# Second block, first pair of down projections: the three product terms outside the contraction tiles

## The reference, cut to what matters

```python
def swiglu(x, w_gate, w_up, w_down):
    return (jax.nn.silu(x @ w_gate) * (x @ w_up)) @ w_down
...
    for l in range(DEPTH_2):
        h = h + 0.5 * swiglu(rmsnorm(h, ffn1_norm[l]), ffn1_w_gate[l], ffn1_w_up[l], ffn1_w_down[l])
        ...
        h = h + 0.5 * swiglu(rmsnorm(h, ffn2_norm[l]), ffn2_w_gate[l], ffn2_w_up[l], ffn2_w_down[l])
```

## Time and profile before

| | |
|---|---|
| median of 3 runs | 3017.49 us (3017.19 to 3018.07) |
| the profiled execution | 3017.36 us |
| its span | 3015.6 us |
| TensorE busy | 2999.4 us |
| VectorE busy | 2122.8 us |
| ScalarE busy | 1449.4 us |
| granted TensorE clock, mean | 0.999 |

### The profile page before, as it was taken

One profiled execution on the slowest core, in us unless ns is written; L12 is line 12 of the kernel. 1 busy time (PEld: TensorE's weight loads), 2 busy tenths in 40 slices (PEclk: granted clock), 3 DMA queues, 4 the chain that ended last, 5 costly groups with the idle time before them and its releaser, 6 DMA issues.

```text
span 3015.6 us, 55700 instructions
## 1 busy us (share of the span) xinstructions
PE 2999.4 (99%) x20562; PEld 2751.3 (91%) x20562; DVE 2122.8 (70%) x3141; ACT 1449.4 (48%) x2555; POOL 190.1 (6%) x237
## 2 busy tenths in 40 slices
PE   9999999999999999999999999999999999999998
PEld 7878887888888899999999999999999999989998
DVE  5545646773576598877667788868887766788876
ACT  4454424442343365634652555536554475356642
POOL 1000000000000011100000011001110000001100
PEclk9999999999999999999999999999999999999999
DMA  4111322222222267533111477336753321257734
GB/s 163 62 64 63 105 98 99 98 97 92 97 97 97 77 181 180 149 109 106 64 64 64 140 178 184 102 112 171 187 147 112 105 71 65 70 148 188 176 105 126
DMA packets 131033, 347.94 MB, mean 115 GB/s; under 512 B 14798, under 2 KB 16334, under 8 KB 130752
## 3 DMA queue, kind: packets, MB, share of 16 engines
q1 hardware_dynamic: 103536, 292.34, 28.8%
q0 software_dynamic: 27056, 53.16, 10.4%
q10 hardware_dynamic: 288, 0.31, 0.0%
HBM read 343.58 MB, written 2.17 MB: 115 GB/s over the span
## 4 chain that ended last, share of the span: by engine, by line
PE 79%; issue 16%; DVE 3%; ACT 1%; POOL 1%; DVEq 1%; DMA 0%; POOLq 0%; SPq 0%; ACTq 0%
PE ps L3129 25%; PE ps L2704 22%; PE ps L2852 9%; PE ps L3194 6%; PE ps L2717 3%; PE ps L3483 3%; PE ps L3176 3%; PE ps L2869 1%; PE ps L2937 1%; PE ps L3261 1%; DVE w_lo L1591 0%; PE ps L2925 0%; PE ps L2906 0%; PE ps L2758 0%; PE ps L2778 0%
## 5 line engine op out<-in xcount | busy, mean ns | idle before, releaser
L865 ACT ACTIVATE w_hi<-w_raw 128x1024 fp32r<-128x1024 f32 (+1 forms) x325 | 340.6, 1048 | 567.7 <-PE ps L2704 255.1
L1591 DVE TENSOR_TENSOR w_lo<-w_raw,w_hi 128x1024 fp32r<-128x1024 f32 (+1 forms) x333 | 403.0, 1210 | 200.0 <-ACT w_hi L865 193.8
L2704 PE MATMUL ps<-h_hi,w_lo 128*128 128x512 f32 (+1 forms) x584 | 215.0, 379 | 0.0
L2704 PE MATMUL ps<-h_hi,w_hi 128*128 128x512 f32 (+1 forms) x584 | 213.8, 377 | 1.1 <-DVE w_lo L1591 0.8
L2704 PE MATMUL ps<-h_lo,w_hi 128*128 128x512 f32 (+1 forms) x584 | 213.9, 377 | 0.0
L1232 ACT ACTIVATE h_spare<-ps 128x264 f32<-128x264 f32 (+1 forms) x304 | 118.2, 389 | 130.0 <-PE ps L3129 129.8
L2852 PE MATMUL ps<-h_hi,w_hi 128*128 128x512 f32 x416 | 168.3, 405 | 0.0
L2852 PE MATMUL ps<-h_hi,w_lo 128*128 128x512 f32 x416 | 163.2, 392 | 0.0
L2852 PE MATMUL ps<-h_lo,w_hi 128*128 128x512 f32 x416 | 163.1, 392 | 0.0
L2704 PE MATMUL ps<-f_hi,w_lo 128*128 128x512 f32 (+1 forms) x520 | 154.4, 338 | 0.0
L2704 PE MATMUL ps<-f_lo,w_hi 128*128 128x512 f32 (+1 forms) x520 | 153.8, 337 | 0.0
(11 more groups left out here) (542 smaller groups left out, 7785.6 us busy)
## 6 DMA issues: line engine op xcount, KB each, us to landing
w_raw<-in_stream SPq DMA_DIRECT2D x384, 512.0 KB, 3.3
s_raw<-in_stream SPq DMA_DIRECT2D x152, 256.0 KB, 4.4
s_raw<-in_stream POOLq DMA_DIRECT2D x152, 256.0 KB, 4.1
tmp<-in_stream SPq DMA_DIRECT2D x76, 256.0 KB, 5.1
w_raw<-in_stream SPq DMA_DIRECT2D x32, 256.0 KB, 2.7
w_mix<-in_stream SPq DMA_DIRECT2D x24, 256.0 KB, 3.4
w_mix<-in_stream SPq DMA_DIRECT2D x12, 512.0 KB, 4.7
w_mix<-in_stream POOLq DMA_DIRECT2D x24, 256.0 KB, 4.6
```

What stands on the lines that cost most here:

```text
L865: nc.scalar.activation(w_hi[:, s, 0:n], w_raw[:, s, 0:n], ACT.Copy).then_inc(hi_done, 1)
L1591: V.tensor_tensor(w_lo[:, s, 0:n], w_raw[:, s, 0:n], w_hi[:, s, 0:n].bitcast(F32), ALU.subtract).then_inc(lo_done, 1)
L2704: last = T.matmul(out[:, p, :], w[:, s, j * P:(j + 1) * P], x[:, k, c0:c1], start=start and j == 0 and r == 0, stop=stop and j == len(ks) ...
```

## The change

The first pair's seven units no longer go through `unit`. The matmuls are written out in `first_unit` with the loops exchanged: the three terms outside, the contraction tiles inside them, the one or two parts innermost as before. The wait for a tile's `f2_lo` stands ahead of the tile's matmul of the first term. The wait for the weights, the matmuls themselves with their operands and banks, and the increment at the end stay as they are.

```diff
                     def f_ready(k):
                         pe.wait_ge(al_done, a0 + f_place(k) + 1)
-                    unit(u0 + FF2_TILES + d // 2, d % 2, bank(at_bank[m], n_tok), F.f2_hi, F.f2_lo, ks, n_tok,
-                         start=ks[0] == 0, stop=ks[-1] == 2 * KT - 1, step=f_ready)
+                    pe.wait_ge(lo_done, down + d + 1)
+                    for r, (w, x) in enumerate(((w_hi, F.f2_hi), (w_hi, F.f2_lo), (w_lo, F.f2_hi))):
+                        for j, k in enumerate(ks):
+                            if r == 0:
+                                f_ready(k)
+                            for p, c0, c1 in parts(n_tok):
+                                last = T.matmul(bank(at_bank[m], n_tok)[:, p, :], w[:, d % 2, j * P:(j + 1) * P], x[:, k, c0:c1],
+                                                start=j == 0 and r == 0 and ks[0] == 0,
+                                                stop=j == len(ks) - 1 and r == 2 and ks[-1] == 2 * KT - 1)
+                    last.then_inc(unit_done, 1)
```

## The result

The changed kernel takes 3026.66 us (median of 9 runs, 3026.27 to 3036.41), the kernel before 3017.65 us in the same session: 9.0 us more, ratio 1.0028 with a 95% interval of 1.0018 to 1.0037. Forecast were 3026.3 us, made of 8.94 us of waits.

The account below looks back on a forecast made before the run. TensorE was taken as the bound, busy 2999.4 of 3015.6 us. Three 528-token calls at 2.19 us (6.57) plus 2.37 for the 512-token call add 8.94 to 3017.36: 3026.3 us, range 3022.5 to 3029.0.

Parts of the forecast that it names:

- No cost of the order: Matmuls in the four calls: new order at most 0.16 us faster by spacing; taken as 0.
- First unit: Each 528-token call: TensorE waits for tile 7's `f2_lo`, 0.76 us late plus 0.11, 0.87 us.
- the restart: First matmul after a wait: next weights not loaded ahead, 0.11 us more for each wait.
- The latency from VectorE's end to the matmul: From the end of a VectorE instruction to the matmul it releases: 0.05 us.
- Fifth unit: Each 528-token call: tile 15 is 1.21 us late, its chain tied to TensorE's progress; 1.32 us with 0.11 added.
- The second rival: Fifth unit: tiles 14 and 15 not tied to TensorE, loss 0.45 instead of 1.32 us; 3022.7 us total, chance 8%.
- The call with 512 tokens: Last call: 0.98 us in its first unit and 1.39 in its fifth, together 2.37 us.
- The other units: Units two to four, six and seven: their tiles are ready in time, no loss.
- the first rival: TensorE waits less later because VectorE gains a lead; given back in full, 3017.4 us; chance 4%.
- the third: Rival: knock-on at the weight split after the seven units, 4.3 us more in all, 3030.6 us; chance 4%.
- The signs that I had named: Profile after: `f_lo` releases TensorE at the new line; calls of 34.2 us (528 tokens), 32.5 (last); spacing 0.121 us away from waits.
- Sum: All four calls: 6.57 + 2.37 = 8.94 us, all on TensorE, giving 3026.3 us.

Follow-up runs that it names:

- e4: Changed kernel with the first and fifth of the seven units back in the old order: 3017.89 us, ratio 1.0004 to the kernel before.
- e5: Changed kernel, all seven units in new order, first term waiting only for upper halves (`f2_hi`), second for `f2_lo`: 3018.20 us, ratio 1.0000.
- e8: Kernel before, contraction tiles outside, terms reordered so weights change three times a tile instead of twice: 3017.65 us, ratio 0.9991.
- e9: Changed kernel with the three terms outside only groups of four contraction tiles: 3017.90 us, ratio 1.0002 to the kernel before.
- e2: Changed kernel with only the fifth unit back in the old order: 3021.36 us, ratio 1.0015 to the kernel before.
- e3: Changed kernel with only the first unit back in the old order: 3022.67 us, ratio 1.0019 to the kernel before.
- e6: Changed kernel with VectorE's weight split for the sixth unit moved behind `f2_lo` of tiles 14 and 15: 3021.74 us, ratio 1.0007.
- e7: As e6, and tile 7's `f2_lo` also moved ahead of a gate sum on VectorE: 3018.45 us, ratio 0.9998 to the kernel before.
- e1: Changed kernel run again without edit, for a second profile: 3027.1 us, ratio 1.0034 to the kernel before.
- e10: Changed kernel with tile 7's `f2_lo` later on VectorE, behind the up sum and gating: 3034.62 us, ratio 1.0057 to the kernel before.

## Why the prediction was right, by its own steps

**No cost of the order.** Held, as far as timings tell: five units in the new order add nothing (e4), nor do seven (e5), nor a third weight change for each tile (e8). I took 0, with a gain of at most 0.16 us as the bound; what the profiles of e5, e8 and e9 show is a loss of some 0.1 us in a call with 528 tokens (32.06 to 32.09 in place of 31.99) and 0.2 in the last (30.42 or 30.43 in place of 30.24), 0.5 us in all, too small for the timings. e8 has it with the tiles outside, so it isn't a price of terms outside; where it comes from is not shown.

**First unit.** Forecast: tile 7 late by 0.76 us and 0.11 for the restart, 0.87; shown: late by 0.78, and 0.89 in all (e2's first call, 32.88 - 31.99), with the pair behind the wait at 0.51 us where undisturbed pairs take 0.40 or 0.41, the 0.11 of the restart. The latency from VectorE's end to the matmul was 0.06 us for 0.05.

**Fifth unit.** Forecast 1.32, shown 1.33 (e3: 33.32 - 31.99). Tile 15 was due at 1308.13 + 14 x 0.1212 = 1309.83 and starts at 1311.04: 1.21 us late, as forecast. That the loss hangs on the fourth unit's end through ScalarE and VectorE, and so doesn't shrink when TensorE is late already, is shown by e3: without the first unit's delay it is the same 1.33 us. The second rival had it at 0.45 when the delay stands before it; both profiles of the changed kernel speak against that. Taking VectorE's link to that end away (e6) leaves 0.96 us of the call's 2.27, little more than the first unit's 0.89.

**The call with 512 tokens.** Forecast 2.37, shown 2.36 up to the next unit. The step held, but my account of it was half of the cause. VectorE is also late by its own work there: ahead of that `w_lo` it idles only 0.34 us for ScalarE in the changed kernel, where it idles 0.68 with 528 tokens, and when the link is cut 0.76 us of the loss stay (e7).

**Everything else.** The other units didn't wait. Nothing was given back: in e1's profile the span grew by 9.1 us and the calls, up to the next unit, by 9.0, so the first rival is out. No wait appeared behind the seventh unit; VectorE's idle time ahead of the last split was 1.49 us (1.48 before), so the third is out too. I had said that it would grow by 1.32, but the growth lies ahead of the split before it (0.38 to 1.73), where it does the same service. The signs that I had named came as well: stretches of 34.25 to 34.27 and 32.58 us where 34.2 and 32.5 were forecast, and the spacing is 0.121 us away from the waits.

**Sum.** 3 x 2.27 + 2.36 = 9.2 by the profiles, 9.0 by the medians, 8.94 forecast.

## What to carry to other kernels

Moving a loop inside out moves the deadline of every operand, even when the matmuls and their number stay: with the terms outside, eight tiles' halves are all wanted within a third of the unit's time. Before such a change, set the new deadline of the last tile against the time at which it is ready, and see whether its producer hangs on the consumer's own progress; if it does, a delay elsewhere buys nothing. If the order is wanted for another reason, let each term wait for what it reads (e5), or exchange the loops only over as many tiles as are ready (e9): neither costs anything here that the timings show.

## What the runs showed of the hardware

*The spacing of matmuls has more than one value at the same granted clock.* The first profile of the changed kernel against the second of the same kernel, L2704 alone (512 columns), ahead of any changed instruction:

```profile
550.00:700.00 150.00, 150.00 (x644) 121.51 (x644) 1.00 0.28 94
```

```profile
550.00:700.00 150.00, 150.00 (x657) 123.07 (x656) 1.00 0.29 97
```

That is 0.233 us a matmul in the one, 0.228 in the other, both never idle and at a granted clock of 1.00. From about 550 to 1070 us it makes 9.4 us. One of the changed kernel's nine runs is so long. The profile of e7, an execution of 3028.1 us, has the same 644 matmuls in this window. The kernel before has executions of 3026.6 to 3027.7 us as well, eight of 35, beside its median of 3018.2 in the same series; none of those was profiled. It also goes the other way: behind the last call, 146 matmuls of 256 columns touch a stretch of 16.20 us in the kernel with the first unit back, where before 145 touch 16.80 us, at the same granted clock. What sets it I have not tried to find. A profile's span alone can mislead by 10 us through it, while the stretches of the calls agreed within 0.07 us in the two profiles of the changed kernel.

*A wait of 2 us can cost more than itself.* In e10 the clock fell behind one wait of 2.02 us and not behind the three others of 2.0 to 2.1 us; it cost 1.45 us in that call. The waits of the change itself, 0.6 to 0.7 us idle, left it at 1.00 in both profiles.
